# Two more buffers for the normed columns, 22-quarter slots for tiles 12 to 14, a spread last tile, and the halo rows turned on TensorE

## What is computed

```python
def layer(x, ...):
    h = rms_norm(x, norm1)
    p = h @ w_in                                  # columns u_a v_a q k v z beta a
    y_a = rms_norm(gmlp_spatial(gelu(u_a), gelu(v_a), gmlp_ws, gmlp_bs))
    qkv_c, new_buf = causal_conv(qkv, conv_buf, conv_w)     # new_buf: the last 3 rows of qkv
    q, k, v = split(silu(qkv_c))                  # then l2norm of q and k
    o, S_new = gated_delta_chunked(q, k, v, g, beta, S0, chunk)
    y_b = rms_norm(o, gdn_norm) * silu(z)
    x = x + concatenate([y_a, y_b]) @ w_o
    h2 = rms_norm(x, norm2)
    x = x + (silu(h2 @ w_gate) * (h2 @ w_up)) @ w_down
```

## Time and profile before

| | |
|---|---|
| measured time, median of 3 | 2801.35 us (2799.75 to 2803.41) |
| the profiled execution, its own time | 2794.26 us |
| its span, first to last instruction | 2792.6 us |
| PE busy | 2717.5 us (97%) |
| DVE, ACT busy | 1408.6 us (50%), 985.2 us (35%) |
| granted TensorE clock, mean | 0.992 of full speed |
| DMA, share of 16 engines | 37.4% |

### The profile page before, as it was taken

The page is one execution under the profiler, slowest core; times in us unless marked ns, Lnnn a source line. Parts: engine busy times, 40 slices in busy tenths (PEclk is TensorE's granted clock), DMA queues, the critical chain, the costliest instruction groups (busy, mean ns, idle before and its releaser), DMA issues.

```text
span 2792.6 us, 46417 instructions
## 1 busy us (share of the span) xinstructions
PE 2717.5 (97%) x19256; PEld 2405.9 (86%) x19256; DVE 1408.6 (50%) x2303; ACT 985.2 (35%) x1634; POOL 21.6 (1%) x60
## 2 busy tenths in 40 slices
PE   8999999999999998699999999999999999999998
PEld 7877777777777776699999999999999998999998
DVE  4566767767666665433343335433334355344344
ACT  3435555656555464312212124121211133222222
POOL 2000000000000000000000000000000000000000
PEclk9999999999999999899999999999999999999999
DMA  9355444445444956622222225222122152222220
GB/s 301 97 162 178 129 130 152 141 121 166 142 121 145 181 183 217 209 61 60 60 75 60 60 83 173 75 60 60 60 60 75 53 174 82 70 77 82 66 75 38
DMA packets 361901, 315.13 MB, mean 113 GB/s; under 512 B 15653, under 2 KB 315762, under 8 KB 359714
## 3 DMA queue, kind: packets, MB, share of 16 engines
q1 hardware_dynamic: 361762, 313.20, 37.4%
HBM read 254.80 MB, written 58.36 MB: 112 GB/s over the span
## 4 chain that ended last, share of the span: by engine, by line
PE 57%; DVE 1%; ACT 1%; issue 0%; DVEq 0%; POOL 0%; ACTq 0%; POOLq 0%
PE gate_ps L2595 7%; PE gate_ps L2597 7%; PE gate_ps L2596 7%; PE up_ps L2595 7%; PE up_ps L2597 6%; PE up_ps L2596 6%; PE down_ps L2595 6%; PE down_ps L2596 6%; PE down_ps L2597 6%; DVE w_in_sb L2589 0%; ACT h_hi L2391 0%; ACT w_hi L2372 0%; DVE w_in_sb L2490 0%; DVE h_lo L2512 0%; DVE w_in_sb L2534 0%
## 5 line engine op out<-in xcount | busy, mean ns | idle before, releaser
L1645 PE MATMUL pr_p<-hT_hi_p,w_hi_p 128*128 128x512 f32 x992 | 421.4, 425 | 7.1 <-DVE hT_lo_p L1086 5.0
L1646 PE MATMUL pr_p<-hT_lo_p,w_hi_p 128*128 128x512 f32 x992 | 389.7, 393 | 0.0
L1647 PE MATMUL pr_p<-hT_hi_p,w_lo_p 128*128 128x512 f32 x992 | 389.6, 393 | 0.0
L2476 DVE TENSOR_TENSOR w_in_sb<-up_ps,w_in_sb 128x384 f32<-128x384 f32 (+1 forms) x132 | 70.7, 536 | 602.7 <-PE up_ps L2597 602.7
L2595 PE MATMUL gate_ps<-h_hi,w_hi 128*128 128x384 f32 (+1 forms) x1056 | 346.1, 328 | 17.1 <-DVE w_lo L2466 14.4
L2597 PE MATMUL gate_ps<-h_hi,w_lo 128*128 128x384 f32 (+1 forms) x1056 | 345.6, 327 | 0.0
L2596 PE MATMUL gate_ps<-h_lo,w_hi 128*128 128x384 f32 (+1 forms) x1056 | 345.5, 327 | 0.0
L2595 PE MATMUL up_ps<-h_hi,w_hi 128*128 128x384 f32 (+1 forms) x1056 | 344.0, 326 | 0.0
L2597 PE MATMUL up_ps<-h_hi,w_lo 128*128 128x384 f32 (+1 forms) x1056 | 343.9, 326 | 0.0
L2596 PE MATMUL up_ps<-h_lo,w_hi 128*128 128x384 f32 (+1 forms) x1056 | 343.9, 326 | 0.0
L2490 DVE TENSOR_TENSOR w_in_sb<-down_ps,w_in_sb 128x1024 f32<-128x1024 f32 x187 | 228.8, 1223 | 183.1 <-PE down_ps L2597 182.2
(11 more groups left out here) (378 smaller groups left out, 4055.6 us busy)
## 6 DMA issues: line engine op xcount, KB each, us to landing
w_in_sb<-in_w_in SPq DMA_DIRECT2D x100, 512.0 KB, 4.4
w_in_sb<-in_w_gate SPq DMA_DIRECT2D x66, 512.0 KB, 4.0
w_in_sb<-in_w_up SPq DMA_DIRECT2D x66, 512.0 KB, 5.2
w_in_sb<-in_w_down SPq DMA_DIRECT2D x33, 1024.0 KB, 4.8
stream_tiles<-w_in_sb SPq DMA_DIRECT2D x96, 256.0 KB, 2.5
w_in_sb<-stream_tiles SPq DMA_DIRECT2D x16, 1280.0 KB, 7.1
w_in_sb<-mixed_tiles SPq DMA_DIRECT2D x29, 512.0 KB, 5.2
out<-w_in_sb SPq DMA_DIRECT2D x21, 512.0 KB, 4.0
```

What stands on the lines that cost most here:

```text
L1645: pe.matmul(out, w_h, x_h, start=start, stop=False)
L1646: pe.matmul(out, w_h, x_l, start=False, stop=False)
L1647: return pe.matmul(out, w_l, x_h, start=False, stop=stop)
L2476: dve.tensor_tensor(act[:, h, 0:half], up_ps[h][:, 0:half], gate_act[:, h, 0:half], ALU.mult)\
```

## The change

It does four things. A function `place(t, stop)` takes the place of the formula above. For tiles up to 11 it is the same. Tiles 12 to 14 get 22 quarters each (`TIGHT`), their stops scaled by 22/25 and rounded down, so that stops 8 and 9 fall together, and 16 and 17. Tile 15 begins at quarter 466, one quarter to a stop up to 20, and two to a stop behind it: solve at 488, outputs at 490, the output norm at 496. The buffers of normed columns become four, by the parity of the tile (`h2_cols`), so `h2_columns` waits for the store of two items before. The halo is turned by one TensorE transpose into `gs` (`turn_halo`, in tile 12 before stop 6), copied by VectorE behind the decayed keys (`copy_halo`), and stored by SP as 12 transfers of 3 rows of 512 B (`store_halo`). SP's slot is put in another order: z, halo, the next streams, and only then the y of the tile before, all at stop 8.

```diff
+        def place(t, stop):
+            if t < DONE:
+                return (t + MACRO) * SLOT + stop
+            at = (DONE + MACRO) * SLOT + (t - DONE) * TIGHT
+            if t < TILES - 1:
+                return at + stop * TIGHT // SLOT
+            return at + stop + max(0, stop - 20)
...
-                while done[0] < (t + MACRO) * SLOT + stop:
+                while done[0] < place(t, stop):
...
-        h2_stored = [sem(f"h2_stored{i}") for i in range(2)]
+        h2_stored = [[sem(f"h2_stored{ring}{i}") for i in range(2)] for ring in range(2)]
+        h2_cols = [[cin[:, i, 0:HC] for i in range(2)], [flat(bs_s[:]), sb("h2_odd", [P, HC])[:]]]
...
-                past(dve, h2_stored[i], 16 * m)
-                dve.tensor_tensor(cin[:, i, 0:HC].rearrange("p (c i) -> p c i", i=P), gs_cols,
+                past(dve, h2_stored[m % 2][i], 16 * (m // 2))
+                dve.tensor_tensor(h2_cols[m % 2][i].rearrange("p (c i) -> p c i", i=P), gs_cols,
...
             def slot(t):
                 upto(t, 2)
-                if t > 0:
-                    store_y(t - 1)
                 if t == TILES - 1:
                     load_h2_ahead(0)
                     load_h2_ahead(1)
                 upto(t, 8)
+                if t >= 0:
+                    load_z(t)
+                    if t == TILES - MACRO:
+                        store_halo()
+                    if (t + 1) % MACRO and t + 1 < TILES:
+                        load_streams(t + 1)
+                if t > 0:
+                    store_y(t - 1)
+                upto(t, 16)
...
+            def store_halo():
+                sp.wait_ge(s["halo_copied"], 1)
+                for x, lo in (("k", D_B), ("q", 0), ("v", 2 * D_B)):
+                    for c in range(4):
+                        at = (CONV_W - 1) * ("kqv".index(x) * 4 + c)
+                        sp.dma_start(a["new_conv"][:, lo + c * P:lo + (c + 1) * P], halo_rows[at:at + CONV_W - 1])\
+                          .then_inc(s["rows_stored"], 16)
...
+            def copy_halo():
+                dve.wait_ge(s["halo_turned"], 1)
+                dve.tensor_copy(halo_rows, gs[0:12 * (CONV_W - 1), 0:P]).then_inc(s["halo_copied"], 1)
...
+            def turn_halo():
+                n = 12 * (CONV_W - 1)
+                pe.wait_ge(s["halo_out"], 12 * MACROS)
+                pe.wait_ge(s["va_ready"], TILES - MACRO + 1)
+                pe.transpose(gs[0:n, 0:P], halo[:].rearrange("p a r -> p (a r)"), sh["ident"][:]).then_inc(s["halo_turned"], 1)
```

More of the change, by code:

```diff
@@ L156, in prompt_phase @@
     SLOT = NI
+    TIGHT = 22
     ITEMS = MACROS * NI
@@ L299, in prompt_phase @@
         gs_cols = gs[:].rearrange("p (t c) -> p t c", t=MACRO)
+        halo_rows = upto_s[0:12 * (CONV_W - 1)]
         gs_small = gs[:, 0:2 * MACRO * H_B].rearrange("p (a t h) -> p a t h", a=2, t=MACRO)
@@ L314, in prompt_phase @@
             o_norm_ready y_ready y_stored s_stored rows_stored mask_step
-            wo_loaded first_added second_added h2_ready""".split()
+            wo_loaded first_added second_added h2_ready halo_turned halo_copied""".split()
         s = {x: sem(x) for x in names}
@@ L480, in store_h2 @@
                 sp.wait_ge(s["h2_ready"], 2 * m + i + 1)
-                sp.dma_start(a["h2t"][m][:, i * HC:(i + 1) * HC], cin[:, i, 0:HC]).then_inc(h2_stored[i], 16)
+                sp.dma_start(a["h2t"][m][:, i * HC:(i + 1) * HC], h2_cols[m % 2][i])\
+                  .then_inc(h2_stored[m % 2][i], 16)
             def quarter(n, part):
@@ L542, in store_y @@
                 sp.dma_start(a["y"][t], yT[:].rearrange("p c i -> p (c i)")).then_inc(s["y_stored"], 16)
+            def store_halo():
[5 more added lines that the diff above has]
+                          .then_inc(s["rows_stored"], 16)
             def load_h2_ahead(i):
                 for half in range(2):
-                    sp.wait_ge(h2_stored[half], 16 * (i + 1))
+                    sp.wait_ge(h2_stored[i % 2][half], 16 * (i // 2 + 1))
                 sp.dma_start(*a["ahead_h2"][i]).then_inc(s["ahead_loaded"], 16)
@@ L560, in slot @@
                     load_h2_ahead(2)
[L561 to L565, removed]
                 if fronted(t) is not None and fronted(t) + 1 < TILES:
@@ L611, in _ @@
                 slot(t)
[L612 to L619, removed]
                 if t == TILES - 2:
@@ L628, in _ @@
             for i in range(2):
-                sp.wait_ge(h2_stored[i], 16 * DONE)
+                for half in range(2):
+                    sp.wait_ge(h2_stored[i][half], 16 * (DONE // 2))
                 sp.wait_ge(row_stored[i], 16 * (DONE // 2))
@@ L1577, in slot @@
                     decayed_keys(t)
+                if t == TILES - MACRO:
+                    copy_halo()
                 if (t + MACRO) % MACRO == 1 and j < MACROS:
@@ L1906, in sum_gates @@
                 last.then_inc(s["small_pe"], 1)
+            def turn_halo():
[3 more added lines that the diff above has]
+                pe.transpose(gs[0:n, 0:P], halo[:].rearrange("p a r -> p (a r)"), sh["ident"][:]).then_inc(s["halo_turned"], 1)
             def turn_va(t):
+                if t > TILES - MACRO:
+                    pe.wait_ge(s["halo_copied"], 1)
                 pe.wait_ge(rc_loaded[t % 2], 16 * (t // 2 + 1))
@@ L2056, in slot @@
                     keys_queries(t)
+                    if t == TILES - MACRO:
+                        upto(t, 6)
+                        turn_halo()
                     upto(t, 8)
```

## The result

The changed kernel takes **2812.22 us** (median of 5, 2810.81 to 2814.29) against 2799.75 for the kernel before on the same chip: ratio 1.0042, 95% interval 1.0031 to 1.0053. It is slower by 12 us; 2795 was forecast, with a range up to 2806. Up to 899 us the two traces agree within 0.1 us, and the second phase, which starts 17.6 us later, is as long within 0.5, so all of it lies between.

What follows compares the result with a forecast made beforehand. PE, with work for 97% of the span, was taken as the bound, with time only in its waits and lower clock. Removing 20.2 us and adding 13.7 gains 6.5, from 2801.35 to 2795 us; forecast's range 2791 to 2798, with rivals 2786 to 2806.

Steps and rivals of the forecast that it cites:

- 3.1 us of new clock terms: Lower PE clock behind new waits in tiles 12 to 14: 1.4, 0.8, 0.4 and 0.5 us; without them, 2792.
- Removed, 16.6 us: Tiles 14 and 15: two buffers a half end VectorE's store waits, giving PE 13.5 us of waits and 3.1 of clock.
- the four VectorE entries, 13.5 us, are one cause: PE's waits for column step, level, scaling and split square all queue behind VectorE's column step waiting for its store.
- second rival: Tile 15: row loads replace stores as what the turn waits for, 2.4 us in seven items; 2812 us, chance 0.13.
- Tile 12's first level, 4.0 us: PE arrives two quarters early but ScalarE's norms do not move: 2.6 us wait and 1.4 of lower clock.
- SP's hold, 3.8 us: SP stands for the halo copy; tile 13's streams reach ScalarE late, so PE waits 3.0 us, plus 0.8 of clock.
- third rival: Halo holds SP longer: 0.71 us an issue gives 2800 us, with streams landing in 13.1 us 2806; chance 0.13.
- The halo leaving its old place, 3.6 us: PE's wait behind the old halo's issues goes: 1.9 us gained, and 1.7 of clock in 965 to 975.
- Tile 13, 1.5 us: Chain from keys to last product shows 1.1 us past PE's own work, and 0.4 where stops 16 and 17 coincide.
- Tile 14, 2.6 us: The quarter with the weight split falls between the same steps as in tile 12: 2.1 us and 0.5 of clock.
- Tile 15, 1.5 us (0 to 4): Begun nine quarters earlier, its steps meet VectorE's column steps of other items; 1.5 us as a rest of lateness.
- The end, 0.3 us: Some 3.5 us of solve, outputs and state move ahead of the last quarter; 0.3 us more on balance.

Runs made afterwards that it cites:

- mends: Changed kernel with halo transfers at stop 16, second-phase weight loads spread and first normed-column loads later, tile 14's GELUs together: 2793.87 us; with tile 12 at 25 quarters, 2784.51.
- wide slots: Changed kernel with 25 quarters again for tiles 12 to 14 and tile 15 at quarter 475: 2792.92 us; with halo transfers moved to stop 16 as well, 2783.13.
- e3: Changed kernel with the second phase's four weight loads one to an item and its first two normed-column loads two quarters later: 2806.8 us, ratio 1.0030.

## Why the prediction was wrong

The prediction had 4.4 us of waiting and 2.1 of lower clock go away on balance; 8.9 of waiting and 9.3 of lower clock came in their place. So some 13 us of the miss are waits and 11 are clock. (Its 3.1 us of new clock terms count tile 13's 0.4, which its own text gives to two steps that fall together; 2.7 are clock.) The steps, one by one:

- **Removed, 16.6 us: mis-sized, and one wait mis-assigned.** Two buffers alone brought 10.6 us (6.7 to 14.3). The step "the four VectorE entries, 13.5 us, are one cause" fails for the longest, 5.4. There the store landed late because four weight loads lay on the rings; with them spread it went though the buffer stayed single, and with two buffers a late row load took its place. That is the second rival's mechanism, in one item instead of seven. For tile 14's 3.3 us the step holds.
- **Tile 12's first level, 4.0 us: right mechanism, the wait right, the clock too small.** ScalarE's norms came forward by 0.04 us only. Of the wait of 4.09, 2.6 are new, as forecast, and the clock took 0.34 x 7.76 = 2.6 us for 1.4: 5.2 in place. Widening tile 12 gave back 13.4 without mends and 10.9 with them, so more followed from it than its own place shows; the prediction took tile 12's lateness as separate from the tiles behind it, and named that as what would make it wrong.
- **SP's hold, 3.8 us: the times right, the path wrong, the size 4.8 here and 9.2 in wide slots.** The twelve issues took 3.74 us for 3.6. But ScalarE did not wait for the streams, as the term has it, since it came to their SiLU late itself. It waited for weights that stood behind the hold as well: 0.92 us here, 8.4 in the run with wide slots. The term had no price for them, so that its size is near 4.8 is luck. The third rival's longer issues did not happen. The Trainium skill, "DMA: Bandwidth & Descriptors", Anatomy of one DMA, says that a semaphore wait is served at the issuing sequencer and not in the DMA engines; the trace agrees, with SP standing 10.5 us for VectorE's copy, everything behind it unissued.
- **The halo leaving its old place, 3.6 us: not shown in time.** The wait behind it is gone from the trace, but the runs with the new halo stored late are not told apart from those with the old one: 0.9946 against 0.9962 for the buffers alone, and 0.9955 against 0.9949 with spread loads, with overlapping intervals.
- **Tile 13, 1.5 us: right** (1.0 and 0.35). **Tile 14, 2.6 us: too small**: the levels waited 1.4, 1.7 and 1.5, with lower clock from 1020 to 1030, and the turn 4.4 for the GELU, because of a norm between two users of one table that no term had.
- **Tile 15, 1.5 us (0 to 4): the term that failed most.** It had one wait of 7.9 us and 1.8 of lower clock behind it. Moving tile 15 nine quarters ahead of the items moved its SP steps past the items' loads: a load of a column tile now follows the store of that tile by 2 us instead of about three items, and item 117's rows are behind it. The prediction traced SP's queue in tile 12 only.
- **The end, 0.3 us: right.**

The second rival's time, 2812, was met by luck: it has a turn wait 2.4 us for a row load in each of seven items, and one turn waited 7.9 us in one item, while the rest came from tiles 12 and 14 and the clock.

The Trainium skill, "TensorE: Matmul & The Clock Gate", Part 1, on the array falling back after idle time, agrees with the windows: a mean of 0.66 behind the waits of 4.1, 4.4 and 7.9 us.

## What to carry to other kernels

A wait that names a store or a load tells which transfer came last, not why it was late: look at what else lies on the same rings and queue in those microseconds before giving the wait a price, since a second buffer then only hands it on. When two hand-woven streams are moved against each other, walk every queue through the whole moved stretch, the transfer queue first; two of the costs here were meetings of single instructions, absent three quarters further on. Removing cover from a chain gains nothing at a place whose input does not come earlier, so first find the engine that sets the input, here ScalarE's table loads at the head of tile 12.

## What the runs showed of the hardware

Twelve transfers of 3 rows of 512 B took SP 3.74 us to issue, against 8.47 for twelve of single floats. Where four loads of 512 KB were issued back to back, SP's issue itself became longer: 0.42 us for the first and 1.09, 2.85 and 1.58 for the others in tile 15, against 0.43 for each of the four in e3, where they were spread. Behind the wait of 4.4 us PE ran at 1.2 GHz from its end at 1049.8 to about 1058 (0.50 in 1050 to 1055), though it was busy throughout from 1050 on; a part of 1040 to 1045 was at 1.2 GHz too (0.66), behind a wait of 1.5 us at a level. The wait for the old halo's twelve transfers varied from trace to trace of kernels that share that place: 1.9, 3.1, 4.6 and 5.5 us at PE.
